# Decode attention: eight score tiles at once, pages turned one step ahead, the fetch one unit further, the maximum in two columns

## The reference, cut to what matters

```python
q_lat = einsum('nthd,chd->nthc', q_nope, w_uk)
s_past = (einsum('nthc,nlc->nhtl', q_lat, past_ckv) + einsum('nthr,nlr->nhtl', q_rope, past_kr)) * MLA_SCALE
...
p = softmax(concatenate([s_past, s_new], axis=-1))
o_lat = einsum('nhtl,nlc->nthc', p[..., :l], past_ckv) + ...
```

## Time and profile before

| what | us |
|---|---|
| median of three runs (lowest, highest) | 3207.59 (3205.59, 3209.54) |
| profiled execution: its time, its span | 3204.92, 3203.1 |
| TensorE busy in the span | 2990.5 |
| VectorE, ScalarE, GpSimd busy | 1808.3, 602.5, 872.5 |

### The profile page before, as it was taken

One profiled execution on the slowest core, in us unless ns is written; L12 is line 12 of the kernel. 1 busy time (PEld: TensorE's weight loads), 2 busy tenths in 40 slices (PEclk: granted clock), 3 DMA queues, 4 the chain that ended last, 5 costly groups with the idle time before them and its releaser, 6 DMA issues. The chain is left out here.

```text
span 3203.1 us, 58513 instructions
## 1 busy us (share of the span) xinstructions
PE 2990.5 (93%) x23093; PEld 2616.2 (82%) x23093; DVE 1808.3 (56%) x2739; ACT 602.5 (19%) x1199; POOL 872.5 (27%) x496
## 2 busy tenths in 40 slices
PE   6967999998999899999999999988889999999996
PEld 6944666665555499999999999985589999999996
DVE  8895655565888635533515345667747515335354
ACT  3111544551000102100000001106512100000011
POOL 3300000100000045434344344420044444443432
PEclk9988999998999899999999999999999999999998
DMA  2100000004777521111111111202111111111112
GB/s 101 54 14 31 15 14 14 0 26 141 228 223 228 149 91 56 46 44 49 47 51 43 42 53 39 69 21 88 53 50 59 41 51 46 41 51 40 52 43 72
DMA packets 129157, 206.34 MB, mean 64 GB/s; under 512 B 14833, under 2 KB 95729, under 8 KB 128274
## 3 DMA queue, kind: packets, MB, share of 16 engines
q1 hardware_dynamic: 90994, 162.31, 16.3%
q10 hardware_dynamic: 38016, 41.99, 4.4%
HBM read 189.87 MB, written 6.25 MB: 61 GB/s over the span
## 5 line engine op out<-in xcount | busy, mean ns | idle before, releaser
L121 POOL TENSOR_TENSOR sb_slab_hi<-sb_slab_raw,sb_ones 128x1024 fp32r<-128x1024 f32 (+3 forms) x214 | 344.7, 1611 | 1716.0 <-PE ps_trunk_out L139 1052.1
L137 PE MATMUL ps_trunk_out<-sb_h_hi,sb_slab_hi 128*128 128x344 f32 x2400 | 769.2, 320 | 0.0
L138 PE MATMUL ps_trunk_out<-sb_h_hi,sb_slab_lo 128*128 128x344 f32 x2400 | 765.8, 319 | 0.0
L139 PE MATMUL ps_trunk_out<-sb_h_lo,sb_slab_hi 128*128 128x344 f32 x2400 | 765.6, 319 | 0.0
L123 POOL TENSOR_TENSOR sb_slab_lo<-sb_slab_raw,sb_slab_hi 128x1024 fp32r<-128x1024 f32 (+3 forms) x214 | 488.5, 2283 | 16.7
L137 PEld LDWEIGHTS ps_trunk_out<-sb_h_hi,sb_slab_hi 128*128 128x128 f32 x2400 | 450.9, 188 | 0.6
L138 PEld LDWEIGHTS ps_trunk_out<-sb_h_hi,sb_slab_lo 128*128 128x128 f32 x2400 | 450.8, 188 | 0.6
L139 PEld LDWEIGHTS ps_trunk_out<-sb_h_lo,sb_slab_hi 128*128 128x128 f32 x2400 | 450.8, 188 | 0.0
L137 PE MATMUL ps_trunk_out<-sb_ffn_a_hi,sb_slab_hi 128*128 128x344 f32 x1056 | 337.4, 319 | 5.0 <-DVEq L1535 5.0
L139 PE MATMUL ps_trunk_out<-sb_ffn_a_lo,sb_slab_hi 128*128 128x344 f32 x1056 | 338.4, 320 | 0.0
L138 PE MATMUL ps_trunk_out<-sb_ffn_a_hi,sb_slab_lo 128*128 128x344 f32 x1056 | 336.6, 319 | 0.0
(11 more groups left out here) (398 smaller groups left out, 4501.8 us busy)
## 6 DMA issues: line engine op xcount, KB each, us to landing
sb_slab_raw<-f_w_gu SPq DMA_DIRECT2D x88, 512.0 KB, 3.5
sb_dec_ck<-cache ACTq DMA_DIRECT2D x256, 144.0 KB, 2.6
sb_dec_ck<-cache SPq DMA_DIRECT2D x256, 144.0 KB, 3.0
sb_slab_raw<-f_w_down SPq DMA_DIRECT2D x32, 384.0 KB, 3.0
sb_slab_raw<-f_w_down SPq DMA_DIRECT2D x32, 320.0 KB, 2.8
sb_slab_raw<-e_w_out SPq DMA_DIRECT2D x24, 256.0 KB, 2.6
sb_slab_raw<-o_w_in SPq DMA_DIRECT2D x12, 512.0 KB, 3.5
sb_slab_raw<-e_w_in SPq DMA_DIRECT2D x10, 512.0 KB, 3.5
```

Source lines behind the costliest of these rows:

```text
L121: nc.gpsimd.tensor_tensor(hi, raw, one, ALU.mult).then_inc(self.hi_done[s], 1)
L137: nc.tensor.matmul(out[:, t, 0:TT], a, x_hi(k)[:, cols], start=k == 0, stop=False)
L138: nc.tensor.matmul(out[:, t, 0:TT], b, x_hi(k)[:, cols], start=False, stop=False)
L139: last = nc.tensor.matmul(out[:, t, 0:TT], a, x_lo(k)[:, cols], start=False, stop=k == kc - 1)
```

## The change

- `scores` does a whole unit: the eight tiles of one block of 32 values, four for each half, are issued together. The second half's tile of quarter b writes output quarter (b + 2) mod 4. Each half has a bank of its own, so scores use banks 0 to 3 and values banks 4 and 5 (2 and 3 before).
- The turns of unit w+2 stand in step w, and `turned` counts units, not halves. The order on VectorE is: maximum of w, group 0 of w+2, probabilities of w, outputs of w-1, groups 1 to 3 of w+2.
- `turn_prob` is three transposes: one of 256 columns on all partitions for the first half, and two of 256 columns on 64 partitions that move the second half's quarters back to their places.
- The maximum is kept in columns 0 and 5 of one tile in turn; a copy from `m_all` begins each sample, and two operations of each unit go (lines 1357 and 1365).
- ScalarE's fetch after unit w is that of w+3, not w+2.

```diff
-                    def scores(w, half):
+                    def scores(w):
...
-                        pe.wait_ge(turned, 2 * w + half + 1)
-                        if w >= 2 and half == 0:
+                        pe.wait_ge(turned, w + 1)
+                        if w >= 2:
                             pe.wait_ge(p_done, w - 1)
-                        x, pages = w % 2, slice(half * UP // 2, (half + 1) * UP // 2)
+                        x = w % 2
                         for j in range(NJ):
-                            for b in range(4):
-                                m = MM(bank[quads[b], x, half * 256:half * 256 + 256], qc[quads[b], (w // NU) % 2, j, :],
-                                       ckT[quads[b], x, pages, 32 * j:32 * j + 32], start=j == 0, stop=j == NJ - 1)
-                        if half:
-                            m.then_inc(s_done, 1)
+                            for half in range(2):
+                                for b in range(4):
+                                    m = MM(bank[quads[(b + 2 * half) % 4], 2 * x + half, 0:256], qc[quads[b], (w // NU) % 2, j, :],
+                                           ckT[quads[b], x, half * UP // 2:(half + 1) * UP // 2, 32 * j:32 * j + 32],
+                                           start=j == 0, stop=j == NJ - 1)
+                        m.then_inc(s_done, 1)
...
-                    scores(0, 0)
+                    scores(0)
+                    own_values()
                     for w in range(WU):
-                        scores(w, 1)
-                        if w == 0:
-                            own_values()
                         if w + 1 < WU:
-                            scores(w + 1, 0)
+                            scores(w + 1)
                         values(w)
...
-                        if w >= 1 and w + CKS - 1 < WU:
-                            fetch_act(act, w + CKS - 1)
+                        if w + CKS < WU:
+                            fetch_act(act, w + CKS)
...
                     def maximum(w):
 
                         n, k = w // NU, slice(w % 2, w % 2 + 1)
-                        old = m_all[:, n:n + 1]
+                        new, old, five = ((0, 5, slice(1, 6)), (5, 0, slice(0, 5)))[w % 2]
+                        mnew, mold = mrun[:, new:new + 1], mrun[:, old:old + 1]
+                        if w % NU == 0:
+                            ch.link(V.tensor_copy(mold, m_all[:, n:n + 1]))
                         dve.wait_ge(s_done, w + 1)
...
-                        ch.link(V.tensor_copy(cmax[0:32, 4:5], m_all[0:32, n:n + 1]))
...
-                        dve.wait_ge(mx_done, w + 1)
-                        V.tensor_tensor(old, mnew[:, :], mnew[:, :], ALU.max)
...
                     def turn_prob(w):
                         dve.wait_ge(p_done, w + 1)
-                        V.transpose(probT[:, w % 2, :], prob[:, w % 2, :]).then_inc(pt_done, 1)
+                        x, low, high = w % 2, slice(0, UP * 16), slice(UP * 16, UP * 32)
+                        V.transpose(probT[:, x, low], prob[:, x, low])
+                        V.transpose(probT[64:128, x, high], prob[0:64, x, high])
+                        V.transpose(probT[0:64, x, high], prob[64:128, x, high]).then_inc(pt_done, 1)
...
+                    turn(1, (0, 1, 2, 3))
                     for w in range(WU):
                         if (w + 1) % NU == 0 and w + 1 < WU:
                             queries((w + 1) // NU)
-                        if w + 1 < WU:
-                            turn(w + 1, (0, 1))
+                        maximum(w)
+                        if w + 2 < WU:
+                            turn(w + 2, (0,))
+                        turn_prob(w)
                         if w:
                             outputs(w - 1)
-                        maximum(w)
-                        if w + 1 < WU:
-                            turn(w + 1, (2,))
-                        turn_prob(w)
-                        if w + 1 < WU:
-                            turn(w + 1, (3,))
+                        if w + 2 < WU:
+                            turn(w + 2, (1, 2, 3))
                     outputs(WU - 1)
```

More of the change, by code:

```diff
@@ L1159, in build @@
             m_all, l_all = sb("dec_m", [P, NS]), sb("dec_l", [P, NS])
-            cmax, mnew = sb("dec_cmax", [P, 5]), sb("dec_mnew", [P, 1])
+            mrun = sb("dec_mrun", [P, 6])
             nbias, drop, decay, rs = (sb("dec_" + n, [P, 2]) for n in ("nbias", "drop", "decay", "rs"))
@@ L1234, in blocks @@
                         return m
-                    def scores(w, half):
-                        if w % NU == 0 and half == 0:
+                    def scores(w):
+                        if w % NU == 0:
                             pe.wait_ge(q_ready, w // NU + 1)
-                        pe.wait_ge(turned, 2 * w + half + 1)
-                        if w >= 2 and half == 0:
+                        pe.wait_ge(turned, w + 1)
+                        if w >= 2:
                             pe.wait_ge(p_done, w - 1)
-                        x, pages = w % 2, slice(half * UP // 2, (half + 1) * UP // 2)
+                        x = w % 2
                         for j in range(NJ):
-                            for b in range(4):
-                                m = MM(bank[quads[b], x, half * 256:half * 256 + 256], qc[quads[b], (w // NU) % 2, j, :],
-                                       ckT[quads[b], x, pages, 32 * j:32 * j + 32], start=j == 0, stop=j == NJ - 1)
-                        if half:
-                            m.then_inc(s_done, 1)
+                            for half in range(2):
[4 more added lines that the diff above has]
+                        m.then_inc(s_done, 1)
                     def values(w):
@@ L1260, in values @@
                                 p = 4 * q + g
-                                m = MM(bank[quads[g], 2 + x, 0:KVL], probT[:, x, 32 * p:32 * p + 32],
+                                m = MM(bank[quads[g], 4 + x, 0:KVL], probT[:, x, 32 * p:32 * p + 32],
                                        ck[:, w % CKS, p, 0:KVL], start=q == 0, stop=q == GP - 1)
                         m.then_inc(pv_done, 1)
-                    scores(0, 0)
+                    scores(0)
+                    own_values()
                     for w in range(WU):
-                        scores(w, 1)
-                        if w == 0:
-                            own_values()
                         if w + 1 < WU:
-                            scores(w + 1, 0)
+                            scores(w + 1)
                         values(w)
@@ L1305, in _ @@
                             act.wait_ge(o_ev, w - 1)
-                        nc.scalar.activation(prob[:, x, :], bank[:, x, :], ACT.Exp, scale=MLA_SCALE, bias=nbias[:, k],
+                        nc.scalar.activation(prob[:, x, :].rearrange("p (a t) -> p a t", a=2), bank[:, 2 * x:2 * x + 2, 0:256], ACT.Exp, scale=MLA_SCALE, bias=nbias[:, k],
                                              accum_out=rs[:, k])
@@ L1331, in turn @@
                                             ck[:, w % CKS, g * GP:(g + 1) * GP, :].rearrange("p a c -> p (a c)"))
-                            if g % 2:
+                            if g == 3:
                                 m.then_inc(turned, 1)
@@ L1351, in maximum @@
                         n, k = w // NU, slice(w % 2, w % 2 + 1)
-                        old = m_all[:, n:n + 1]
+                        new, old, five = ((0, 5, slice(1, 6)), (5, 0, slice(0, 5)))[w % 2]
+                        mnew, mold = mrun[:, new:new + 1], mrun[:, old:old + 1]
+                        if w % NU == 0:
+                            ch.link(V.tensor_copy(mold, m_all[:, n:n + 1]))
                         dve.wait_ge(s_done, w + 1)
-                        ch.link(V.tensor_reduce(cmax[:, 0:1], bank[:, w % 2, :], AX, ALU.max))
+                        ch.link(V.tensor_reduce(mrun[:, 1:2], bank[:, 2 * (w % 2):2 * (w % 2) + 2, 0:256], mybir.AxisListType.XY,
+                                                ALU.max))
@@ L1355, in maximum @@
                         for b in range(1, 4):
-                            V.tensor_copy(cmax[0:32, b:b + 1], cmax[quads[b], 0:1])
-                        ch.link(V.tensor_copy(cmax[0:32, 4:5], m_all[0:32, n:n + 1]))
-                        ch.link(V.tensor_reduce(mnew[0:32, :], cmax[0:32, :], AX, ALU.max))
+                            m = V.tensor_copy(mrun[0:32, 1 + b:2 + b], mrun[quads[b], 1:2])
+                        ch.link(m)
+                        ch.link(V.tensor_reduce(mrun[0:32, new:new + 1], mrun[0:32, five], AX, ALU.max))
@@ L1359, in maximum @@
                         for b in range(1, 4):
-                            m = V.tensor_copy(mnew[quads[b], :], mnew[0:32, :])
+                            m = V.tensor_copy(mrun[quads[b], new:new + 1], mrun[0:32, new:new + 1])
                         ch.link(m)
-                        V.tensor_tensor(drop[:, k], old, mnew[:, :], ALU.subtract)
```

(9 more changed lines are left out.)

## The result

The changed kernel takes 3210.83 us (median of 20 runs, 3207.07 to 3225.38), the kernel before, beside it, 3206.42 (20 runs, 3204.45 to 3209.74): a ratio of 1.0018, 95% interval 1.0011 to 1.0024. That is slower, and clear of noise, but at 0.18% it is less than the 0.2% that the prediction called no change (the interval's upper end is just above it).

A forecast was written before the change was run, and what follows sets the result against it. TensorE was taken as the present bound, ScalarE's queue as the next. +7.8 - 3.5 - 6.9 + 5.1 = +2.5 us on 3204.92 gives 3207.4; the median, 2.67 higher, gives 3210, range 3191 to 3236.

The forecast's parts named there:

- The bound: Decode attention loop: TensorE bounds it now; scores fall to 4.1 us, its sum per unit from 9.9 to 6.0 us.
- VectorE: VectorE's work per unit: maximum 2.38 to 2.04 us, three transposes 1.35, sum 9.4 against the present period of 10.55.
- the chain: Loop from exponential through transposes, values and eight page issues to the next exponential: 10.83 us a unit, +7.8 us in all.
- ScalarE's queue: Page issues waiting for a unit's values hold back the next exponential on ScalarE's queue, giving a period of 10.83 us.
- The wait for pages that was called hidden: VectorE's first turn of pages in a unit: pages land at 9.3 us, needed by 10.4, hidden by about 1 us.
- the burst: ScalarE's eight page DMA issues after a unit's values: 6.49 us in all, between 6.05 and 7.65.
- The clock: TensorE's pauses in the loop drop its clock; values at half clock cost 1.7 us each, three units, +5.1 us.
- Start and end: Decode attention stage: exponential 1 comes 3.5 us sooner, and the end after exponential 29 is 6.9 us shorter.
- Eight tiles not side by side: Rival, scores on TensorE: they stay at 8 us, 11.7 us a unit, 3238 us; chance 0.10.
- the queue does not hold: Rival, ScalarE: its queue does not hold the next exponential, VectorE bounds at 9.4 us, 3165 us; chance 0.05.
- Short bursts: Rival, ScalarE's page issues: bursts at 6.05 to 6.15 us, or overlapping transposes, -12 to -19, 3191 to 3198; chance 0.17.
- Values at half clock: Rival, TensorE's values in the loop: ten to 28 units at half clock, +12 to +43, 3222 to 3253; chance 0.18.

The follow-up runs named there:

- the filled pauses: The changed kernel with idle products of 128 columns on TensorE, six before the values and eight after: 3209.85 us, ratio 1.0007.

## Why the prediction was right

**The bound.** Right. TensorE's sum fell as worked out: 4.12 us of scores (4.1 was taken). By the rule of the Trainium skill, "TensorE: Matmul & The Clock Gate", Part 3: Packing small matmuls — row/col tiling, read strictly, they would have stayed near 8; two tiles share each row group here, and the trace with its 4.12 us disagrees. The run with four tiles, at 7.16 and more, puts the gain on the eight.

**VectorE.** Right: three transposes at 1.35 in sequence, from the eight copies that had gained nothing by overlap. The saving on the maximum was taken to be worth nothing in the end, since that part of VectorE's work is not in the chain; the run with the old maximum shows it.

**ScalarE's queue.** Right, and the step that carries the answer: the waits, the timeline, and the time gained, by the ratios, by taking two issues (26 us) and two transposes (15 us) out of the chain. A fourth buffer for pages, which would take the wait itself away, was not tried. That the late fetch costs little while TensorE takes 10.55 us a unit is shown by the run of it alone (0.1%). The wait for pages that was called hidden stayed hidden: VectorE waits 12 times for pages, 18.0 us in all, yet the first transpose begins 0.90 or 0.91 us after the exponential in all 28 units. The terms measured, as means of 28 units, were 0.90 + 1.35 + 0.05 + 1.93 + 0.07 + 6.51 + 0.12 = 10.93 against 10.83: the burst was forecast at 6.49, and the hand-overs at 0.05 each were too short by 0.09 in sum. 28 × (10.93 - 10.55) = 10.6; with 0.66 of late scores in one unit this is the +11.2.

**The clock.** The mechanism was there; the number of units was mis-sized: seven units in the profiled execution, not three, +8.2 for +5.1. That execution lies 4.3 us above the median, and the filled pauses gained less at the median than the 8.2 us in it, so the +4.4 by medians tests the whole sum (+2.5) but not this term.

**Start and end** were within 0.5 us. The 1.7 us after the stage were not foreseen, and the change has no visible part in them. The stage ends 8.5 us later than before; by 1283 us of the kernel before the lag is 7.3, and so it still is at 1960. It grows to 10.2 only in the stage between 2170 and 2320, which the change does not touch; 1.5 of that is one group of 64 small matmuls, before and after:

```profile
2307.43 3.74 PE L1976 MATMUL ps_swa_bank<-sb_z,sb_slab_raw 64*128 64x4 f32 x64 [0.71 <-PEq L1763]
```

```profile
2315.97 5.23 PE L1980 MATMUL ps_swa_bank<-sb_z,sb_slab_raw 64*128 64x4 f32 x64 [0.72 <-PEq L1767]
```

The granted clock was 1.00 throughout the first and 0.50 from 2318 on in the second. Why it fell there was not tested.

**Luck.** That 3210.83 came out beside a forecast of 3210 is in part luck. Between the two profiled executions the sum was +10.2 for +2.5: the chain was 3.4 too short, the clock 3.1 too cheap, the later stages 1.7, start and end 0.6 the other way. All of this is less than the 18 us over which the changed kernel's runs spread, and the kernel before was 1.2 us faster in the runs beside it than in the three of the forecast.

**Rivals.** "Eight tiles not side by side" and "the queue does not hold" are refuted by the 4.12 us and by the waits. "Short bursts" did not come: the shortest are 6.1 us, counted as in the forecast, the mean 6.5. (Its lower end was added up wrong: with bursts of 6.05 and overlapping transposes at once the forecast's own figures, +7.8 to -13.7, give -21.5 and not -19.) "Values at half clock" came in part. The failed expectation is behind the prediction, not in it: removing the chain was to bring a period of VectorE's 9.4 us, and brought 10.2 to 10.5, since pages and the exponential stand right behind.

## What to carry to other kernels

A DMA issue on a compute engine's queue is work of that engine, and one that waits for the end of a step stands ahead of the next step's first instruction: add it up as a link of the loop's chain before moving it. Halving the bounding engine's work gives only the distance to the next chain; write that chain down with every link, among them those that the old bound covered. Where two chains lie within a few per cent, shortening one turns its wait into another, and a table of waits that names one releaser can name the wrong one: compare the ends of both candidates with the start of what waited.

## What was not expected of the hardware

A transfer's issue costs ScalarE's queue the same for 72 KB as for 144 KB: bursts of six took 3.9 and 4.8 us with either size, 4.1 and 4.2 in the mean. Eight tiles, two of them on each row group, run float32 matmuls of 256 columns at 4.12 / 144 = 0.029 us an instruction, a little less than the 0.031 of 64 instructions with eight columns. And idle products that held the clock at 1.00 for the whole loop, where it was 0.88, moved the median by 1 us.
